# A decoder layer on one core: two gate quarters loaded and split inside the expert stage, an embedding product in plain fp32, and one signal fewer

## The reference

```python
x = _layer_norm(DEEPNORM_ALPHA * x + mix, ln1_g, ln1_b)
ffn = _hierarchical_moe(x, ...)        # 32 experts, 2 per token
x = _layer_norm(DEEPNORM_ALPHA * x + ffn, ln2_g, ln2_b)
return x + jax.nn.sigmoid(x @ ple_gate_w) * (p_i @ ple_proj_w)
```

## Time and profile before

| | us |
|---|---|
| median of 3 runs | 762.86 (760.48 to 764.89) |
| profiled execution | 763.6 |
| its span | 761.8 |
| PE busy in the span | 653.7 (86%) |
| DVE busy | 341.2 (45%) |
| ACT busy | 181.3 (24%) |
| POOL busy | 217.8 (29%) |
| mean granted clock of PE | 0.931 |

### The profile page before, as it was taken

The page is one execution under the profiler, slowest core; times in us unless marked ns, Lnnn a source line. Parts: engine busy times, 40 slices in busy tenths (PEclk is TensorE's granted clock), DMA queues, the critical chain, the costliest instruction groups (busy, mean ns, idle before and its releaser), DMA issues.

```text
span 761.8 us, 10052 instructions
## 1 busy us (share of the span) xinstructions
PE 653.7 (86%) x3798; PEld 462.7 (61%) x3798; DVE 341.2 (45%) x791; ACT 181.3 (24%) x346; POOL 217.8 (29%) x179
## 2 busy tenths in 40 slices
PE   4999639999999999799636999999999978771997
PEld 3767527797797787688524555555555534350776
DVE  3389995282283264635862211111211111139933
ACT  4265012422422312610110111111111101150230
POOL 6215401520540420551103333333333331133300
PEclk9969769999999999899876999999999999985899
DMA  6402300230130050057296878999999999555002
GB/s 248 157 1 83 139 0 0 68 127 1 55 111 1 1 221 0 2 191 321 101 395 252 313 287 338 419 415 414 416 413 415 413 416 418 231 225 219 1 28 83
DMA packets 30438, 151.21 MB, mean 198 GB/s; under 512 B 7308, under 2 KB 7564, under 8 KB 16432
## 3 DMA queue, kind: packets, MB, share of 16 engines
q1 hardware_dynamic: 23984, 142.08, 47.3%
q0 software_dynamic: 6400, 8.42, 3.1%
HBM read 148.36 MB, written 14.68 MB: 214 GB/s over the span
## 4 chain that ended last, share of the span: by engine, by line
PE 57%; DVE 11%; DMA 6%; SPq 5%; issue 3%; ACT 1%; POOL 0%; POOLq 0%; DVEq 0%; ACTq 0%
PE bank L1805 14%; PE bank L1514 8%; PE bank L1515 8%; PE bank L1516 8%; PE bank L1820 7%; SPq L419 5%; DMA raw<-in_w_exp_dram 4%; PE bank L1594 3%; PE bank L1795 2%; PE bank L1603 2%; PE bank L1615 2%; DVE res L1489 2%; DVE res L1098 1%; PE bank L1644 1%; DMA pair_dram<-rows_x,row_put 1%
## 5 line engine op out<-in xcount | busy, mean ns | idle before, releaser
L1514 PE MATMUL bank<-w_hi,a_hi 128*128 128x512 f32 (+1 forms) x272 | 104.3, 383 | 9.4 <-DVE w_lo L1480 6.3
L1515 PE MATMUL bank<-w_lo,a_hi 128*128 128x512 f32 (+1 forms) x272 | 102.3, 376 | 0.0
L1516 PE MATMUL bank<-w_hi,a_lo 128*128 128x512 f32 (+1 forms) x272 | 102.0, 375 | 0.0
L1443 DVE COPY rows_x<-bank 128x128 f32<-128x128 f32 x40 | 11.7, 292 | 197.1 <-PE bank L1812 99.3
L625 POOL DMA_INDIRECT pair_dram<-rows_x,row_put x40 | 40.5, 1013 | 167.0 <-ACT rows_x L871 167.0
L1514 PE MATMUL bank<-a_hi,w_hi 128*128 128x512 f32 (+1 forms) x176 | 71.0, 403 | 11.3 <-POOL w_lo L535 9.9
L535 POOL TENSOR_TENSOR w_lo<-raw,w_hi 128x1024 fp32r<-128x1024 f32 x19 | 45.2, 2381 | 121.3 <-ACT w_hi L679 121.2
L1805 PE MATMUL bank<-raw,rows_x 128*64 128x256 f32 x544 | 64.7, 389 | 6.8 <-DMA raw<-in_w_exp_dram 5.3
L1515 PE MATMUL bank<-a_lo,w_hi 128*128 128x512 f32 (+1 forms) x176 | 69.1, 392 | 0.0
L1516 PE MATMUL bank<-a_hi,w_lo 128*128 128x512 f32 (+1 forms) x176 | 68.9, 391 | 0.0
L1514 PEld LDWEIGHTS bank<-w_hi,a_hi 128*128 128x128 f32 x272 | 53.4, 196 | 22.1 <-DVE w_lo L1480 7.2
(11 more groups left out here) (240 smaller groups left out, 1009.4 us busy)
## 6 DMA issues: line engine op xcount, KB each, us to landing
raw<-in_w_exp_dram SPq DMA_DIRECT2D x42, 1024.0 KB
slots<-in_w_exp_dram SPq DMA_DIRECT2D x36, 1024.0 KB
rows_x<-in_w_exp_dram SPq DMA_DIRECT2D x12, 1024.0 KB
raw<-in_w_in_dram SPq DMA_DIRECT2D x19, 512.0 KB, 3.7
raw<-in_w_wide_dram SPq DMA_DIRECT2D x4, 1536.0 KB, 6.7
y<-in_w_exp_dram SPq DMA_DIRECT2D x6, 1024.0 KB
raw<-in_w_out_dram SPq DMA_DIRECT2D x4, 1024.0 KB, 7.9
raw<-pair_dram SPq DMA_DIRECT2D x4, 1024.0 KB, 8.3
```

The lines of the kernel that those rows point to most:

```text
L1514: t_.matmul(o, lh, rh, start=first, stop=False)
L1515: t_.matmul(o, lh, rl, start=False, stop=False)
L1516: return t_.matmul(o, ll, rh, start=False, stop=last)
```

## The change

1. Quarters 0 and 1 of the gate weights are loaded inside the expert stage, by SyncE, into the two pieces of the fifth place that the third last expert frees (`gate_raw`), as soon as its gate and up products have read them. ScalarE rounds them behind its last `put_out`, and VectorE (before: GpSimd) makes their low parts behind its last `copy_hidden`; both ahead of the branch.
2. SyncE itself waits for all scatters (`s_put`) at the end of the expert stage, ahead of its branch, and goes on to the pair loads; `s_landed` is gone. The pair loads come now ahead of everything but quarters 0 and 1; quarters 2 and 3 follow them.
3. The embedding product is made from `p_raw` and `proj_raw` as they are, in fp32, without halves, 16 products of 128x128 by 128x512 into all eight banks. TensorE waits for ScalarE's last copy of the experts (`s_outa`) ahead of its branch, and not for low parts. The four operations that made the halves are gone.
4. `ple` moves to `raw` and the sigmoid's results (`sig`) to `pa`, where `ple` was.
5. In the loop for fuller experts, which isn't run here, two places of weights (`LATER`) are used instead of four.

```diff
-        ple = pa[:, 0:4096].rearrange("p (t c) -> p t c", t=NT)
+        ple = raw[:, 0:4096].rearrange("p (t c) -> p t c", t=NT)
...
+        gate_raw = [pieces[SLOTS][0], pieces[SLOTS][1], y_flat[:, 0:GW], y_flat[:, GW:2 * GW]]
...
+        sig = pa[:, 0:4096].rearrange("p (t c) -> p t c", t=NT)
...
                 sp.wait_ge(s_dn, LAST[NE - RINGS - 1] + 1)
                 load(before, (NE - 1) % RINGS, 2)
+
+                for q in range(2):
+                    sp.wait_ge(s_gu, 2 * LAST[NE - 3] + q + 1)
+                    sp.dma_start(gate_raw[q], d["ple_gate"][q, :, :]).then_inc(s_quarter[q], 16)
                 sp.wait_ge(s_gu, 2 * ITEMS)
                 sp.wait_ge(s_dn, ITEMS)
+                for s in range(4):
+                    sp.wait_ge(s_put[s], 4 * ITEMS)
...
             expert_blocks(sp, run)
 
-            for q in range(2):
-                sp.dma_start(raw[:, q * GW:(q + 1) * GW], d["ple_gate"][q, :, :]).then_inc(s_quarter[q], 16)
-            sp.wait_ge(s_landed, 1)
             for t in range(NT):
                 sp.dma_start(pair_of(t), pair_dram.rearrange("(k t p) c -> t p k c", k=2, p=P)[t, :, :, :])\
                     .then_inc(s_pair[t], 16)
...
             expert_blocks(pool, run)
-            g.sem_inc(s_landed, 1)
-
-            def split_gate(q):
-                pool.wait_ge(s_ghi, q + 1)
...
-            split_gate(0)
-            split_gate(1)
+
             for t in range(NT):
                 inverse(t, s_ve2, s_rs2)
-            split_gate(2)
+            pool.wait_ge(s_ghi, 3)
+            g.tensor_tensor(group(w_lo, OSLOT[2]), gate_raw[2].rearrange("p (u c) -> p u c", u=4),
+                            group(w_hi, OSLOT[2]).bitcast(F32), ALU.subtract).then_inc(s_glo, 1)
...
                     put_out(ITEMS - 1, (ITEMS - 1) % 4)
+                    round_gate(0)
+                    round_gate(1)
                     return
...
-            act.wait_ge(s_pr, 16)
-            a.activation(a_hi[:, 0:2, :], p_raw, ACT.Copy).then_inc(s_phi, 1)
-            act.wait_ge(s_pw, 16)
-            a.activation(w_hi[:, 0:GW], proj_raw, ACT.Copy).then_inc(s_phi, 1)
-            round_gate(0)
-            act.wait_ge(s_plo, 2)
             for u in range(2 * NT):
-                if u == 4:
-                    round_gate(1)
                 ple_out(u)
+            act.wait_ge(s_glo, 2)
...
                     copy_hidden(ITEMS - 1)
+                    for q in range(2):
+                        dve.wait_ge(s_ghi, q + 1)
+                        v.tensor_tensor(group(w_lo, OSLOT[q]), gate_raw[q].rearrange("p (u c) -> p u c", u=4),
+                                        group(w_hi, OSLOT[q]).bitcast(F32), ALU.subtract).then_inc(s_glo, 1)
                     return
...
-            dve.wait_ge(s_phi, 1)
-            v.tensor_tensor(a_lo[:, 0:2, :], p_raw, a_hi[:, 0:2, :].bitcast(F32), ALU.subtract).then_inc(s_plo, 1)
-            dve.wait_ge(s_phi, 2)
-            v.tensor_tensor(w_lo[:, 0:GW], proj_raw, w_hi[:, 0:GW].bitcast(F32), ALU.subtract).then_inc(s_plo, 1)
...
                     down(ITEMS - 1, (ITEMS - 1) % 2, landed(NE - 1), (NE - 1) % RINGS)
+                    pe.wait_ge(s_outa, ITEMS)
                     return
...
-            pe.wait_ge(s_plo, 2)
+            pe.wait_ge(s_pr, 16)
+            pe.wait_ge(s_pw, 16)
+            weights = proj_raw.rearrange("p (u c) -> p u c", u=4)
             for u in range(2 * NT):
                 t, half = u // 2, u % 2
-                if u >= 4:
-                    pe.wait_ge(s_pev, u - 3)
                 for k in range(2):
-                    mm = three(bank[u % 4][:, :], a_hi[:, k, t * P:(t + 1) * P], a_lo[:, k, t * P:(t + 1) * P],
-                               group(w_hi, 0)[:, 2 * half + k, :], group(w_lo, 0)[:, 2 * half + k, :],
-                               k == 0, k == 1)
+                    mm = t_.matmul(bank[u][:, :], p_raw[:, k, t * P:(t + 1) * P], weights[:, 2 * half + k, :],
+                                   start=k == 0, stop=k == 1)
                 mm.then_inc(s_pp, 1)
```

More of the change, by code:

```diff
@@ L48 @@
 RINGS = 5
+LATER = 2
 USED = [len(range(s, NE, RINGS)) for s in range(RINGS)]
@@ L360, in landed_later @@
         def landed_later(first, e, s):
-            return arrived(first + e, s, SLOTS) + 16 * USED[s]
+            return arrived(first + e, s % LATER, LATER) + 16 * USED[s % LATER]
         def arrived(T, par, ring):
@@ L464, in run @@
                     return
-                for s in range(SLOTS):
+                for s in range(LATER):
                     for q in range(3):
@@ L471, in ahead @@
                         wait_count(sp, s_gu, 2 * (base + e) + q + 1)
-                        load(e + SLOTS, s, q)
+                        load(e + LATER, s, q)
                     if known != 0:
                         wait_count(sp, s_dn, base + e)
-                        load(e + SLOTS - 1, (s - 1) % SLOTS, 2)
-                for e in range(SLOTS):
+                        load(e + LATER - 1, (s - 1) % LATER, 2)
+                for e in range(LATER):
                     ahead(e, e, e)
[L479 to L483, removed]
+                with sp.Fori(1, NE // LATER - 1) as i:
+                    for s in range(LATER):
+                        ahead(LATER * i + s, s, None)
+                wait_count(sp, s_dn, base + NE - LATER)
+                load(NE - 1, LATER - 1, 2)
                 wait_count(sp, s_gu, 2 * (base + NE))
                 wait_count(sp, s_dn, base + NE)
+                for s in range(4):
+                    wait_count(sp, s_put[s], 4 * (base + NE))
             expert_blocks(sp, run)
-            for q in range(2):
-                sp.dma_start(raw[:, q * GW:(q + 1) * GW], d["ple_gate"][q, :, :]).then_inc(s_quarter[q], 16)
-            sp.wait_ge(s_landed, 1)
             for t in range(NT):
@@ L495, in _ @@
             for q in range(2, 4):
-                sp.dma_start(y_flat[:, (q - 2) * GW:(q - 1) * GW], d["ple_gate"][q, :, :]).then_inc(s_quarter[q], 16)
+                sp.dma_start(gate_raw[q], d["ple_gate"][q, :, :]).then_inc(s_quarter[q], 16)
             for u in range(2 * NT):
@@ L500, in _ @@
                 sp.dma_start(out[t * P:(t + 1) * P, half * 512:(half + 1) * 512],
-                             raw[:, t * DM + half * 512:t * DM + (half + 1) * 512]).then_inc(s_out, 16)
+                             sig[:, t, half * 512:(half + 1) * 512]).then_inc(s_out, 16)
             sp.wait_ge(s_out, 16 * 2 * NT)
@@ L859, in ple_out @@
                 act.wait_ge(s_pp, u + 1)
-                a.activation(ple[:, u // 2, (u % 2) * 512:(u % 2 + 1) * 512], bank[u % 4][:, :], ACT.Copy)\
+                a.activation(ple[:, u // 2, (u % 2) * 512:(u % 2 + 1) * 512], bank[u][:, :], ACT.Copy)\
                     .then_inc(s_pev, 1)
@@ L871, in put_out, with round_gate @@
                 a.activation(y_out[s], bank[4 + s % 2][:, :], ACT.Copy).then_inc(s_outa, 1)
+            def round_gate(q):
+                act.wait_ge(s_quarter[q], 32)
+                if q == 3:
+                    act.wait_ge(s_gt, NT)
+                a.activation(group(w_hi, OSLOT[q]), gate_raw[q].rearrange("p (u c) -> p u c", u=4), ACT.Copy)\
+                    .then_inc(s_ghi, 1)
             def run(b, base, first):
@@ L921, in _ @@
                 act.wait_ge(s_gt, u + 1)
-                a.activation(raw[:, t * DM + half * 512:t * DM + (half + 1) * 512],
-                             bank[4 * (1 - half) + t][:, :], ACT.Sigmoid).then_inc(s_sig, 1)
+                a.activation(sig[:, t, half * 512:(half + 1) * 512], bank[4 * (1 - half) + t][:, :], ACT.Sigmoid)\
+                    .then_inc(s_sig, 1)
         @block.vector
@@ L1502, in _ @@
                 dve.wait_ge(s_sig, u + 1)
-                o = raw[:, t * DM + half * 512:t * DM + (half + 1) * 512]
+                o = sig[:, t, half * 512:(half + 1) * 512]
                 v.tensor_tensor(o, o, ple[:, t, half * 512:(half + 1) * 512], ALU.mult).then_inc(s_mix, 1)
@@ L1845, in step @@
                 def step(e, s, known):
-                    gate_up(base + e, s % 2, landed_later(first, e, s), s)
+                    gate_up(base + e, s % 2, landed_later(first, e, s), s % LATER)
                     if known != 0:
@@ L1851, in step @@
                     if known != 0:
-                        down(base + e - 1, 1 - s % 2, landed_later(first, e - 1, (s - 1) % SLOTS), (s - 1) % SLOTS)
+                        down(base + e - 1, 1 - s % 2, landed_later(first, e - 1, (s - 1) % SLOTS), (s - 1) % LATER)
                 block_items(pe, step)
                 turn_hidden(base + NE - 1)
-                down(base + NE - 1, 1, landed_later(first, NE - 1, SLOTS - 1), SLOTS - 1)
+                down(base + NE - 1, 1, landed_later(first, NE - 1, SLOTS - 1), LATER - 1)
+                wait_count(pe, s_outa, base + NE)
             expert_blocks(pe, run)
-            pe.wait_ge(s_plo, 2)
+            pe.wait_ge(s_pr, 16)
```

(9 more changed lines are left out.)

13 lines of the change are left out of this document (1 added, 12 removed).

## The result

The changed kernel takes 753.35 us (median of 4 runs, 750.55 to 756.49), the kernel before beside it 763.88 (4 runs). The ratio is 0.986, with a 95% interval of 0.983 to 0.9895: 8 to 13 us faster. Measured again later beside 11 runs of the kernel before (763.87), it took 754.66, a ratio of 0.988 (0.985 to 0.991). The forecast was 752.0, in a range of 749.0 to 758.5.

What follows compares the result with a forecast made beforehand. The bound was taken to be the chain from the last expert scatter to VectorE's first addition; savings of 5.3 (scatter), 2.1 (hop) and 3.9 (addition) sum to 11.3 us off 763.6, forecast 752.0, range 749.0 to 758.5.

Steps and rivals of the forecast that it cites:

- The quarters move for nothing: Quarter loads queued behind expert weights: no cost to experts, second landed near 668, VectorE's added work covered by 0 to 1.3 us.
- The last scatter: Last expert scatter, no longer sharing DMA engines with the quarters: 3.1 us instead of 8.13, saving 5.3 us.
- The hop: From scatter seen to first pair load, SyncE waiting itself instead of through GpSimd: 1.28 us instead of 3.41, saving 2.1.
- The first addition: VectorE's first addition of a pair, without GpSimd's differences beside it: 1.3 us instead of 5.18, saving 3.9.
- The embedding product: TensorE's 16 fp32 products: 14.1 to 15.7 us, from 667.8 to about 682.5, hidden before the first transposes at 688.2.
- (a): Quarters still collide with the last scatter, which stays slow: gain 6.0 us, 757.6; chance 0.14 together with (f).
- (b): Quarters delay the last expert's weights by 5.05 us in the DMA queue: gain 6.2 us, 757.4; chance 0.05.
- (c): First addition slow for another reason, such as pairs written to SBUF, stays 5.18 us: gain 7.4, 756.2; chance 0.05.
- (d): TensorE's clock stays up (0.7 us) and the scatter takes its lower 2.4 us (0.7 more): 750.6; chance 0.09.
- (e): TensorE's clock doesn't come back in the gate product, costing 25 us for half the tail: 777; chance 0.02.
- (f): Quarters don't land early, about 672 as now, so the scatter stays slow: gain 6.0 us; chance 0.14 with (a).

Runs made afterwards that it cites:

- Experiment 1: Changed kernel with the loads of quarters 0 and 1 issued only behind the last expert product, as late as before: 758.27 us.
- experiment 6: Kernel before with the hop alone taken away, SyncE waiting for the scatters itself and issuing the pair loads: 761.38 us.
- experiment 7: Kernel before with only the low parts of quarters 0 and 1 made by VectorE instead of GpSimd: 760.67 us.
- experiment 2: Changed kernel with the low parts of quarters 0 and 1 made by GpSimd behind its branch again, loads still early: 758.61 us.
- kernel 9: Changed kernel with SyncE's scatter and TensorE's last-copy waits behind the branch, first pair in two DMAs, VectorE's scalings before its differences: 751.09 us, ratio 0.983.

## Why the prediction was right

**The quarters move for nothing.** Right. They are issued at 640.69; the last expert's halves start 2.4 us apart, as before, and from the third last expert's second half to the last one's it is 15.5 us in both (641.10 to 656.64, before 643.19 to 658.68). The second is there at 666.83, 10.2 us behind the start of the tail; I had 668 − 658.7 = 9.3. VectorE was ready at 673.5, 1.8 us ahead of the pair, where I had allowed 0 to 1.3: its queue had read the count while the subtraction ran (1.3), and the pair came 0.5 later behind the start of the tail than I had it. Experiment 1 shows the other side: with quarters late, this path and the pair are late together.

**The last scatter.** Right, 4.9 for 5.3, and experiment 1 gives the cause. That a DMA engine alternates between its queues, as the page "DMA: Bandwidth & Descriptors" of the Trainium skill has it (Queues, rings and completion order), fits: 3.45 us with 0.2 of the engines busy or less, 7.5 with the quarters issued just before. Which engine was last no row shows. My 3.1 may have been short because the quarters' traffic, which ends at 667, is still there at its issue (stretches of 1 us, columns as in the earlier trace rows):

```profile
665.00:666.00 1.00, 0.00 (x0) 0.00 (x0) 0.00 (x0) 1.00 (x1) 0.73 (x1) 1.00 0.19 78
666.00:667.00 1.00, 0.00 (x0) 0.00 (x0) 0.67 (x1) 0.46 (x2) 0.25 (x1) 0.70 0.22 66
667.00:668.00 1.00, 0.00 (x0) 0.00 (x0) 1.00 (x1) 1.00 (x1) 0.00 (x0) 0.50 0.03 4
```

**The hop.** Right: 2.2 for 2.1, by the same two steps of SyncE as measured before. I took it as a term of its own; experiment 6 shows that alone, with GpSimd's differences where they were, it is worth 0.4 at most.

**The first addition.** Right, 3.9, and shown from both sides: 1.29 in the kernel before without GpSimd's operations (experiment 7), 3.71 and 5.43 in the changed kernel with them (experiment 2). That GpSimd and VectorE contend where VectorE has two SBUF inputs is what the page "GPSIMD Engine Reference" of the Trainium skill (Key points) says. The rows of GpSimd's 128x2048 differences agree; beside its 128x1 operations nothing is to be seen of it (679.75, 1.55 us long, with VectorE's two additions at 679.59 taking 2.60 together). The prediction says that the first addition ended when the differences did; it ended 1.1 us behind them (689.43 and 688.34).

**The embedding product.** Right that it is hidden, wrong in the place: I had it from 667.8 to 682.5 with 5.7 us of cover left, it had 0.7. Two steps failed. I gave TensorE SyncE's 1.28 us for count and branch, and it takes 4.7 (664.5 to 669.22), of which its branch alone is 3.48. It showed in the kernel before as well, where the wait for the low parts covered it; I hadn't looked at the branch's line. And in this gap, 5.35 us long, the granted clock fell to 0.50 at 666 to 667 and was back at 673 to 674 (mean 0.88), so the first 4 us of the product ran at half speed: 15.96 us in all, where 16 products at full speed are 13.8. Behind the start of the tail the product began 3.5 us late and took 1.3 longer than I had it, the tile was ready 0.3 later, and the last copy behind the product (0.6) I hadn't counted: 5.7 − 3.5 − 1.3 + 0.3 − 0.6 = 0.6. The branch on each engine (ns min/median/max, first and last start):

```profile
L346 PEldq COMPARE_BRANCH  x1: 3479/3479/3479, 665.6 to 665.6; - x1
L346 ACTq COMPARE_BRANCH  x1: 45/45/45, 667.6 to 667.6; - x1
L346 SPq COMPARE_BRANCH  x1: 58/58/58, 669.4 to 669.4; - x1
```

**The rivals.** (a) and (b) are out by the changed kernel itself, (c) by experiments 2 and 7. (d), a clock that stays up through the idle time before the transposes, came in part: it is at full speed for the first transposes (1.06 us instead of 1.94), but falls in the 5.63 us behind them, so that the second take 1.97 as before, and comes back at 697.1, 3.8 us after these begin instead of 5.8. TensorE so takes the last tile when it is ready (708.17), where before it came 0.7 late (721.63), but it then waits for VectorE's low part (L1216): the product behind those transposes starts 16.0 us behind the second ones instead of 16.3. That is the 0.2 us of the last line of the table. The shorter scatter of (d), 2.4 us, didn't come. (e) didn't happen. (f) didn't either, but experiment 1 is its case, and shows what it left out: it lets both quarters land at 672, where ScalarE begins with the first; in experiment 1 the second came 3.7 us behind the first (676.24, 672.50), so that the low parts weren't ready ahead of the pair but with it. That 11.3 were forecast and 11.0 found rests on small errors, 0.4 and 0.2 lost, 0.1 and 0.2 gained; the medians say 10.5 and 9.2.

## What to carry to other kernels

Follow the chain across the border of two stages: the last store of one and the first load of the next are often the path, and whatever else is issued beside them lengthens it; move such loads to where the queue is full anyway. Take the elementwise work that runs beside VectorE's critical additions off GpSimd before shortening a wait ahead of them, or the earlier start is swallowed. Put a wait behind a branch, not ahead of it, when the branch doesn't depend on it: here this took 1.1 us off the path for no work. Look up the branch in every engine's queue, not in one, before you price it.

## What the runs showed of the hardware

- The same branch, its body not run, costs 45 to 72 ns on ScalarE, SyncE, VectorE and GpSimd, but on TensorE 3.4 to 4.0 us in eleven of the twelve profiled executions and 6.65 us in experiment 1, where it began (669.13) 1.5 us behind the issue of the two quarters. GpSimd loses 2.5 to 2.9 us directly behind it, where SyncE loses 0.44. The page "Runtime: NRT & Kernel Launch" of the Trainium skill (Instruction fetch mechanics) says that a taken branch to a target outside what is fetched waits for a fetch. The traces agree: the profile counts DMA queues of kind "instruction", and in all twelve one 16 KB packet of such a queue (q8) starts while TensorE is in its branch, which ends 2.4 to 2.9 us behind the packet's start. It starts 0.9 to 1.5 us into the branch, but 4.2 us into it in experiment 1, with the quarters on the engines. In GpSimd's gap of 2.50 us in the kernel before, a packet of such a queue (q14) is the only DMA traffic. No experiment takes the fetch away, so that it is the cause is read from these times, not tested. The DMA queues during TensorE's branch (packets, MB, share of 16 engines), in the changed kernel and in experiment 1:

```profile
q1 hardware_dynamic: 7, 0.03, 2.3%
q8 instruction: 1, 0.02, 1.8%
...
q1 hardware_dynamic: 274, 1.98, 71.9%
...
q8 instruction: 1, 0.02, 0.9%
```

- GpSimd's subtraction of 128x2048 and a VectorE operation with two inputs in SBUF (1.3 us alone) wait for each other. In all seven pairs read here VectorE's operation ended 1.1 us behind GpSimd's, and so took 3.7 to 5.4 us by how early it had begun. GpSimd's took 4.5 to 4.6 us, and 5.4 to 5.5 where such an operation of VectorE was under way when it began. One pair is left in the changed kernel, between the two rows below; TensorE is busy for 4.90 of the 5 us from 705 to 710, so little can be had from it now.

```profile
700.30 5.41 POOL L668 TENSOR_TENSOR w_lo<-y,w_hi 128x2048 fp32r<-128x2048 f32 x1
...
702.44 4.37 DVE res L1207
```

- A plain fp32 product of 128x128 by 128x512 took 0.86 us at full clock: ScalarE's copies, one for every two products, follow each other at 1.72 us (673.86, 675.58 and 677.29 in kernel 9).
